# First expert's first weight chunks: rounded earlier on ScalarE, two of their rests made on GpSimd

## What is computed

```python
h2 = rms_norm(x, lp['norm2_g']) * (1.0 + scale2) + shift2
x = x + gate2 * expert_choice_moe(h2, ...)

def expert_choice_moe(h, w_router, w_gate, w_up, w_down):
    cap = max(1, EC_CAPACITY_FACTOR * N // N_EXPERTS)      # 64 latent, 16 context tokens for each expert
    aff = jax.nn.softmax((h @ w_router).astype(jnp.float32), axis=-1)
    gates, idx = lax.top_k(aff.transpose(0, 2, 1), cap)
    # for each of 16 experts: xe = h[idx]; silu(xe @ w_gate) * (xe @ w_up) @ w_down, times gates, added at idx
```

## Time and profile before

| | |
|---|---|
| median of 3 runs | 1917.66 us (1912.48, 1917.66, 1917.73) |
| the profiled execution | 1913.52 us, of it a span of 1911.4 us |
| TensorE busy | 1791.8 us, 94% |
| VectorE busy | 1432.3 us, 75% |
| ScalarE busy | 1111.0 us, 58% |
| GpSimd busy | 400.5 us, 21% |
| granted TensorE clock, mean | 0.972 |
| DMA | 511.36 MB, mean 268 GB/s |

### The profile page before, as it was taken

How to read it: one execution, slowest core, us unless ns; L and a number is a source line. 1 busy time by engine, 2 the same in 40 slices (tenths; PEclk the granted TensorE clock), 3 DMA queues, 4 the chain that set the end, 5 groups by cost and what they waited for, 6 DMA issues and landing times.

```text
span 1911.4 us, 23962 instructions
## 1 busy us (share of the span) xinstructions
PE 1791.8 (94%) x8609; PEld 1267.9 (66%) x8609; DVE 1432.3 (75%) x1394; ACT 1111.0 (58%) x1161; POOL 400.5 (21%) x220
## 2 busy tenths in 40 slices
PE   5899999999788879499999999999999999999996
PEld 2687778777677767266666666666666666666664
DVE  1599326123577756789998998998999889899994
ACT  2443222222577731277777777777777777777773
POOL 1266303000011100103303311320330331132021
PEclk9899999999799999599999999999999999999998
DMA  9233734352222222599999999999999999999993
GB/s 331 89 122 127 264 131 168 117 201 89 84 67 67 67 81 85 172 346 375 383 383 379 380 386 380 379 383 380 371 382 383 379 378 385 375 379 384 382 374 114
DMA packets 270913, 511.36 MB, mean 268 GB/s; under 512 B 10572, under 2 KB 35364, under 8 KB 270856
## 3 DMA queue, kind: packets, MB, share of 16 engines
q1 hardware_dynamic: 261496, 486.00, 70.5%
q0 software_dynamic: 9360, 24.60, 4.6%
HBM read 488.52 MB, written 22.04 MB: 267 GB/s over the span
## 4 chain that ended last, share of the span: by engine, by line
PE 81%; DVE 6%; POOL 4%; DMA 3%; ACT 2%; issue 2%; SPq 1%; DVEq 0%; ACTq 0%; POOLq 0%
PE banks L1441 25%; PE banks L1442 25%; PE banks L1443 24%; POOL qk_swp L1337 2%; PE banks L1600 2%; POOL qk_swp L1332 1%; DMA v_h<-v_scr 1%; DMA raw<-in_w_ada 1%; PE banks L1460 1%; PE banks L1696 1%; PE banks L1572 1%; DVE w_lo L880 1%; PE banks L1663 1%; DVE nbias L1105 1%; DVE qk_raw L970 1%
## 5 line engine op out<-in xcount | busy, mean ns | idle before, releaser
L1290 DVE TENSOR_TENSOR w_lo<-raw_x,w_hi 128x2048 fp32r<-128x2048 f32 x192 | 437.4, 2285 | 65.2 <-ACT w_hi L858 63.4
L1290 DVE TENSOR_TENSOR w_lo<-raw,w_hi 128x2048 fp32r<-128x2048 f32 x189 | 430.9, 2287 | 35.2 <-ACT w_hi L858 31.5
L858 ACT ACTIVATE w_hi<-raw 128x2048 fp32r<-128x2048 f32 x189 | 362.9, 1920 | 110.6 <-PE banks L1443 108.3
L858 ACT ACTIVATE w_hi<-raw_x 128x2048 fp32r<-128x2048 f32 x192 | 368.0, 1917 | 85.5 <-PE banks L1443 84.0
L1441 PE MATMUL banks<-w_hi,xe_hi 128*80 128x512 f32 x1024 | 405.8, 396 | 2.2 <-issue 2.2
L1442 PE MATMUL banks<-w_hi,xe_lo 128*80 128x512 f32 x1024 | 403.8, 394 | 0.0
L1443 PE MATMUL banks<-w_lo,xe_hi 128*80 128x512 f32 x1024 | 400.0, 391 | 0.0
L1417 POOL DMA_INDIRECT out<-yeg,idx_l x32 | 146.4, 4574 | 831.6 <-DVE yeg L1252 831.6
L1441 PE MATMUL banks<-w_hi,h_hi 128*128 128x512 f32 x560 | 222.0, 396 | 2.3 <-POOL h_lo L1324 2.3
L1442 PE MATMUL banks<-w_hi,h_lo 128*128 128x512 f32 x560 | 219.5, 392 | 0.0
L1443 PE MATMUL banks<-w_lo,h_hi 128*128 128x512 f32 x560 | 219.0, 391 | 0.0
(11 more groups left out here) (203 smaller groups left out, 2190.7 us busy)
## 6 DMA issues: line engine op xcount, KB each, us to landing
raw<-in_w_gate_e SPq DMA_DIRECT2D x80, 1024.0 KB, 7.7
raw_x<-in_w_down_e SPq DMA_DIRECT2D x80, 1024.0 KB, 8.1
raw<-in_w_up_e SPq DMA_DIRECT2D x64, 1024.0 KB, 7.7
raw_x<-in_w_up_e SPq DMA_DIRECT2D x64, 1024.0 KB, 7.6
raw_x<-in_w_gate_e SPq DMA_DIRECT2D x48, 1024.0 KB, 6.4
raw<-in_w_down_e SPq DMA_DIRECT2D x48, 1024.0 KB, 8.1
raw<-in_w_in SPq DMA_DIRECT2D x28, 1024.0 KB, 6.1
raw<-in_w_ada SPq DMA_DIRECT2D x24, 1024.0 KB, 7.5
```

The costliest lines, as they stand in the source:

```text
L858: nc.scalar.activation(w_hi[:, j % NSPLIT], raw_slot(slot), ACT.Copy).then_inc(hi_done, 1)
L1290: nc.vector.tensor_tensor(w_lo[:, j % NSPLIT], raw_slot(EXPERT_SLOT[j % NRAWE]), w_hi[:, j % NSPLIT], ALU.subtract).then_inc(lo_done, 1)
```

## The change

ScalarE rounds the three chunks directly behind the root of the context tile's mean square (step N of tile 4), ahead of the last exponential, and no longer behind the table. GpSimd makes the first two rests, behind its four copies and ahead of the first gather. VectorE's two are taken out, and its third gets a wait for GpSimd's two.

```diff
                     take_root(roots[0], 1, t)
                     roots[0] += 1
+                    if t == NL:
+                        for i in range(NRAW):
+                            hi(PRE + i)
                 elif what == "A":
...
-            for i in range(NRAW):
-                hi(PRE + i)
-
-
             act.wait_ge(p2_emptied, N_P2)
...
             dve.wait_ge(p2_emptied, N_P2)
-            for i in range(NRAW - 1):
-                lo(PRE + i)
-
             def col(a, x):
...
                 tokens_lo(0, half)
+            dve.wait_ge(lo_done, NSP + NRAW - 1)
             lo(PRE + NRAW - 1)
...
                 nc.gpsimd.tensor_copy(out[:, :, CAP_L:CAP], src[:, :, 1:2].broadcast_to([P, KT, CAP_C])).then_inc(ampx_ready, 1)
+
+            for i in range(NRAW - 1):
+                n = PRE + i
+                pool.wait_ge(hi_done, NSP + i + 1)
+                nc.gpsimd.tensor_tensor(w_lo[:, i], raw[:, n % NRAW], w_hi[:, i], ALU.subtract).then_inc(lo_done, 1)
```

## The result

| | before | after |
|---|---|---|
| median | 1913.66 us (19 runs) | 1919.5 us (19 runs) |
| ratio | | 1.0032, 95% interval 1.0026 to 1.0038 |
| span of the profiled execution | 1911.4 us | 1918.9 us |
| mean granted TensorE clock in it | 0.972 | 0.962 |
| GpSimd busy | 400.5 us | 407.4 us |

The change costs 0.32%, about 6.1 us (5.0 to 7.3); the two medians lie 5.8 us apart. The two errors have opposite signs, so the absolute forecast is nearer than its two parts.

What follows compares the result with a forecast made beforehand. The prediction took TensorE to bound the expert phase, so only the start of its first matmul counts. Held instructions +8.7 and gather -4.1 gave +4.6 us, 1922.3 us against the 1917.66 median, range 1914.0 to 1927.0.

Steps and rivals of the forecast that it cites:

- The two errors: Whole kernel: the absolute forecast was 2.8 us too high, the forecast difference of +4.6 us was 1.5 us too small.
- the absolute forecast: Whole kernel: 1922.3 us, the +4.6 us set on the three-run median of 1917.66 us.
- The ground it stood on: Expert phase, 806 to 1895 us: bound by TensorE, so it only moves with its first matmul, unchanged at 1089 us.
- The two rests: VectorE from 792.56 us, 4.49 us in all: they lie under the first gather, so removing them gives 0 us by itself.
- the early roundings: ScalarE from about 774.6 to 780.1 us: they fit ahead of the exponential due at 787.05, so cost 0 us.
- The held instructions: Context tile's root on VectorE: two two-input instructions each wait for a 4.55 us GpSimd subtraction, making the path 8.7 us late.
- the rival that one-element instructions are not held: Context tile's root: only xn's scaling is held, to 781.1 us; sum -0.2 us, 1917.5 us; chance 0.14.
- The gather: First gather: with VectorE idle and loads nearly over, it lands in 4.6 us instead of 8.72, 4.1 us gained.
- the 0.5 charged: First gather: estimated cost in us of sharing the DMA engines with the weight loads for up to 1.8 us.
- The rival by the rule of the Trainium skill: First gather: issue stays 2.68 us, landing after 6.2 us, only 2.5 us gained; sum +6.2, 1923.9 us; chance 0.08.
- the sum: Up to the first expert matmul: +8.7 us for held instructions, -4.1 us for the gather, +4.6 us in all.

Runs made afterwards that it cites:

- e1_round_only: The change without its GpSimd part: only ScalarE's three roundings moved ahead, both rests left on VectorE; ratio 0.9998 to the kernel before.
- e4_quarters: The change with each GpSimd subtraction cut into four of 128x512; ratio 1.0001 to the kernel before.
- e3_loads_late: The kernel before, with SyncE's expert loads held until the first gather has landed; ratio 0.9991 to the kernel before.
- e10_xn_loads_late: The change, with GpSimd's subtractions waiting for the context tile's xn and SyncE's expert loads for the first gather's landing; ratio 0.9988 to the kernel before.
- e6_one_rest: The change with only the first rest on GpSimd, the second made by VectorE behind gate_c; ratio 1.0017 to the kernel before.
- e11_warm: e10_xn_loads_late plus 12 unused TensorE matmuls between the index transposes and the gathered tokens' transposes; ratio 0.9968 to the kernel before.
- e12_warm_through: e11_warm plus one unused matmul behind the first half of the gathered tokens' transposes and five behind the second; 1904.83 us, 0.9953 of the kernel before.

## Why the prediction was right

**The ground it stood on held.** The expert phase moved as a block, TensorE busy for all of its 1089 us. The two rests had been covered, and the early roundings cost nothing (e1_round_only).

**The held instructions: right in place and mechanism, 0.35 us over in size.** The second instruction with two inputs, the first to start behind GpSimd's start, was held, the one-input one passed, the next two-input one was held again, as written ahead: 8.34 us for 8.7. The subtraction takes 4.5 us, from 4.55 reckoned off 128x128 and 128x640. Nearly half of the 0.35 is the 0.16 us that I let GpSimd's second subtraction wait for VectorE's instruction: its two take 8.97 us together, 778.64 to 787.61, with no pause between. With the two holds fell the rival that one-element instructions are not held, which no row of before could exclude. The rule of the Trainium skill (SBUF — State Buffer, § Who interferes with whom) that a VectorE instruction with two SBUF inputs contends with a GpSimd one that reads SBUF, and that single-input ones outside the two-port modes do not, agrees with the trace down to one element per partition. What it says of the two-port modes, which it names for `tensor_scalar`, fits the scaling in e4_quarters, held for 1.0 us; that the scaling ran in such a mode, no run here shows.

**The gather: landing 4.96 for 4.6 reckoned, 3.8 us gained for 4.1.** The overlap with the end of the weight loads was reckoned well (their last packet ended 3.2 us behind the start of the gather's issue, for 2.9 forecast) but cost 0.9 to 1.1 us over a quiet gather (3.84 to 4.09), not the 0.5 charged. The issue fell to 0.98 us. The rival by the rule of the Trainium skill (SBUF — State Buffer, § Who interferes with whom: `tensor_tensor` leaves descriptor writing alone) is refuted by e3_loads_late and e10_xn_loads_late: 2.68 us beside VectorE's rests, 0.98 without, with nothing else there. Whether it is the writing of descriptors that waits or the reading of the indices from SBUF, no run separates.

**Some luck in the sum.** The held instructions cost 0.35 us less than reckoned and the gather gained 0.35 us less. The two cancel, so the +4.6 us up to the first expert matmul is closer than its terms.

**What was missing: +0.8 us.** The sum ended at the first expert matmul. Four more matmuls at half speed belong behind it in this execution; in other kernels the count varied from 6 to 14 without a pattern, so this term has a size but no certain sign. With it the execution accounts for 5.4 us, inside the measured 5.0 to 7.3.

**The verdict.** I named 0.71 for a change within 0.3% and 0.26 for slower by more. Measured is 1.0032, its interval 1.0026 to 1.0038 on both sides of that line. With 4.6 us as the centre and 5.75 as the line, a term of 0.8 us of either sign mattered: it didn't belong in the centre, but it should have widened the spread, and with it the chance of a loss over 0.3%. The absolute forecast was too high since it took the median of three runs, when the profiled execution's own 1913.52 lay near the median of nineteen.

## What to carry to other kernels

Before work goes to GpSimd "in parallel", list VectorE's instructions in that window by their SBUF inputs: here one with two inputs, of one element per partition, waited for the rest of the GpSimd subtraction that ran, and a chain of them waited once for each subtraction that was ready. A wide `tensor_scalar` with one input was held too (1.73 us for 0.75 in e4_quarters), so count those as well. Start GpSimd behind such a chain, or cut its instruction into pieces. And look at what a gather on the critical path has beside it: keeping weight loads and VectorE's wide subtractions away from it gave 4.6 us from root to matmul here (2.3 in the medians), while the two rests that the change moved had been covered and could give nothing by themselves.

## What the runs showed of the hardware that I had not expected

- A `tensor_tensor` of 128x1 took 4.44 us behind a GpSimd subtraction of 4.5 us, and the `tensor_scalar` of 128x1 between two of these 0.15.
- VectorE's two-input subtraction lengthens GpSimd's issue of an indirect DMA from 0.98 to 2.68 us; one of 2.29 us is enough (e6_one_rest), and the issue ends 0.86 us behind the end of the one that ran when it began.
- Two 1 MB loads beside a gather of 80 rows of 4 KB add 3 to 4 us to its landing.
- TensorE's granted clock rose from 0.50 to 1.00 behind 12 matmuls in the wait (5.2 us at the lower level, 1.2 GHz). It had fallen again at the first matmul after a pause of 2.18 us in e11_warm, and had not after one of 0.98 us, with six more matmuls ahead of it, in e12_warm_through, where no matmul of the experts ran at the lower level.
